# Linear attention's score and output products in another order: lower and upper 64 rows of the array take turns

## The reference, cut to what matters

```
att = jnp.einsum('bthk,bshk,btshk->bhts', qc, kc, jnp.exp(rel))
o = jnp.einsum('bhts,bshv->bthv', att, vc) + jnp.einsum('bthk,bhkv->bthv', qc * jnp.exp(cum), s)
```

## Time and profile before

| | |
|---|---|
| median of 3 runs | 1804.55 us (1803.39 to 1806.12) |
| span of the profiled execution | 1801.9 us |
| PE busy | 1703.9 us (95%), 10222 records |
| PEld busy | 1453.3 us (81%) |
| DVE busy | 1345.6 us (75%) |
| ACT busy | 847.1 us (47%) |
| moved by all transfers | 245.90 MB, mean 136 GB/s |

### The profile page before, as it was taken

How to read it: one execution, slowest core, us unless ns; L and a number is a source line. 1 busy time by engine, 2 the same in 40 slices (tenths; PEclk the granted TensorE clock), 3 DMA queues, 4 the chain that set the end, 5 groups by cost and what they waited for, 6 DMA issues and landing times. The chain is left out here.

```text
span 1801.9 us, 26476 instructions
## 1 busy us (share of the span) xinstructions
PE 1703.9 (95%) x10222; PEld 1453.3 (81%) x10222; DVE 1345.6 (75%) x2521; ACT 847.1 (47%) x1476; POOL 55.0 (3%) x113
## 2 busy tenths in 40 slices
PE   4899999898999999999999998999998999999997
PEld 3788887676888888877788766988898888989997
DVE  6677874775999999977975578699975555765594
ACT  2623334745444442245553565333344467665541
POOL 0910000000000000000000000000000000000000
PEclk9999999999999999999999999999999999999998
DMA  8343432031222225743453332554455454444552
GB/s 318 118 143 115 130 128 70 1 125 63 94 94 95 97 97 195 246 158 117 159 182 115 120 106 95 176 175 152 152 187 190 135 179 143 129 129 129 152 160 87
DMA packets 70150, 245.90 MB, mean 136 GB/s; under 512 B 7951, under 2 KB 9480, under 8 KB 69768
## 3 DMA queue, kind: packets, MB, share of 16 engines
q1 hardware_dynamic: 68024, 241.52, 41.2%
q10 hardware_dynamic: 2000, 2.69, 0.5%
HBM read 242.80 MB, written 1.11 MB: 135 GB/s over the span
## 5 line engine op out<-in xcount | busy, mean ns | idle before, releaser
L462 PE MATMUL banks<-m,weights_high 128*128 128x256 f32 (+1 forms) x4336 | 1042.3, 334 | 33.1 <-DVE weights_low L498 24.9
L462 PEld LDWEIGHTS banks<-m,weights_high 128*128 128x128 f32 x4336 | 734.9, 191 | 125.3 <-issue 23.3
L462 PE MATMUL banks<-m,weights_low 128*128 128x256 f32 (+1 forms) x2168 | 715.3, 330 | 0.0
L498 DVE TENSOR_TENSOR weights_low<-weight_ring,weights_high 128x1024 fp32r<-128x1024 f32 x293 | 355.8, 1224 | 225.1 <-ACT weights_high L493 224.1
L462 PEld LDWEIGHTS banks<-m,weights_low 128*128 128x128 f32 x2168 | 414.2, 191 | 38.3
L493 ACT ACTIVATE weights_high<-weight_ring 128x1024 fp32r<-128x1024 f32 x293 | 308.9, 1056 | 233.7 <-PE banks L462 153.2
L630 DVE SCALAR_TENSOR_TENSOR m<-m,columns 128x189 f32<-128x189 f32 (+4 forms) x856 | 322.0, 456 | 25.0 <-ACT m L570 24.9
L769 DVE SCALAR_TENSOR_TENSOR m<-weight_ring,m 128x1024 bf16<-128x1024 f32 x184 | 225.2, 1224 | 17.9 <-DMA weight_ring<-in_weights 12.1
L569 ACT ACTIVATE m<-banks,columns 128x512 f32<-128x512 f32 (+1 forms) x120 | 83.1, 692 | 305.3 <-PE banks L462 305.2
L462 PE MATMUL banks<-m,weight_ring 128*128 128x256 f32 x704 | 152.1, 379 | 0.0
L462 PEld LDWEIGHTS banks<-m,weight_ring 128*128 128x128 f32 x704 | 133.9, 190 | 17.9
(11 more groups left out here) (393 smaller groups left out, 1600.7 us busy)
## 6 DMA issues: line engine op xcount, KB each, us to landing
weight_ring<-in_weights SPq DMA_DIRECT2D x433, 512.0 KB, 3.7
m<-entering SPq DMA_DIRECT2D x32, 256.0 KB, 3.2
x<-in_tokens SPq DMA_DIRECT2D x1, 2048.0 KB, 13.9
m<-in_cmp_w SPq DMA_DIRECT2D x1, 2048.0 KB, 7.4
m<-in_cond SPq DMA_DIRECT2D x2, 512.0 KB, 4.7
out<-x ACTq DMA_DIRECT2D x8, 128.0 KB, 1.9
columns<-in_columns SPq DMA_DIRECT2D x1, 633.0 KB
m<-in_rg_w ACTq DMA_DIRECT2D x1, 512.0 KB, 3.4
```

Source lines behind the costliest of these rows:

```text
L462: mm = pe.matmul(out, lhsT, rhs, start=p.start and i == 0, stop=p.stop and i == len(passes) - 1)
L498: dve.tensor_tensor(w_lo[:, g % PARTS, :], K.ring[:, PLACE[PRODUCT_BLOCKS[g]] % RING, :], w_hi[:, g % PARTS, :].bitcast(F32), ALU.subtract ...
```

## The change

The score products of one call are issued in two halves of eight. Within a half each product of the lower rows is followed by the one of the upper rows of the same chunk and pair, which goes into the next bank. The output products are issued for each chunk and pair of heads: first the two products over 128 rows, one for each head, then the state's products, lower and upper rows by turns. The products themselves, their operands, the places they write, the semaphores and all other engines' code are the same; the accumulation in each place begins with the same product as before.

```
         def scores(q, k):
-            for i in range(4):
-                r = slice(GK * (i % 2), GK * (i % 2) + GK)
+            for half in range(2):
                 for j in range(4):
-                    c, pair = 2 * (i // 2) + j // 2, j % 2
-                    mm = pe.matmul(K.bank[:, B + i, j * P:j * P + P], k[r, pair, c * P:c * P + P],
-                                   q[r, pair, c * P:c * P + P], start=True, stop=True)
+                    c, pair = 2 * half + j // 2, j % 2
+                    for i in range(2):
+                        r = slice(GK * i, GK * i + GK)
+                        mm = pe.matmul(K.bank[:, B + 2 * half + i, j * P:j * P + P], k[r, pair, c * P:c * P + P],
+                                       q[r, pair, c * P:c * P + P], start=True, stop=True)
             mm.then_inc(*self.scored.up())
...
             for c in (2 * half, 2 * half + 1):
-                for h in range(GH):
-                    mms = [(self.att[:, 4 * (h % 2 + 2 * (c // 2)) + 2 * (c % 2) + h // 2, :],
-                            f["gv"][:, c, h * GV:h * GV + GV])]
-                    r = slice(GK * (h % 2), GK * (h % 2) + GK)
-                    for d in range(2):
-                        pos = CHUNK_ORDER[d].index(c)
-                        if pos:
-                            i = 2 * d + h // 2
-                            mms.append((self.qc[r, i, c * P:c * P + P], self.state[r, i, pos - 1, :]))
-                    for j, (a, b) in enumerate(mms):
-                        at = (2 * (c % 2) + h // 2) * GV
-                        mm = pe.matmul(K.bank[:, B + 2 * half + h % 2, at:at + GV], a, b, start=(j == 0),
-                                       stop=(j == len(mms) - 1))
+                entered = [(d, CHUNK_ORDER[d].index(c) - 1) for d in range(2) if CHUNK_ORDER[d].index(c)]
+                for pair in range(2):
+                    at = (2 * (c % 2) + pair) * GV
+                    outs = [K.bank[:, B + 2 * half + u, at:at + GV] for u in range(2)]
+                    for u in range(2):
+                        h = 2 * pair + u
+                        mm = pe.matmul(outs[u], self.att[:, 4 * (u + 2 * (c // 2)) + 2 * (c % 2) + pair, :],
+                                       f["gv"][:, c, h * GV:h * GV + GV], start=True, stop=not entered)
+                    for n, (d, pos) in enumerate(entered):
+                        for u in range(2):
+                            r = slice(GK * u, GK * u + GK)
+                            mm = pe.matmul(outs[u], self.qc[r, 2 * d + pair, c * P:c * P + P],
+                                           self.state[r, 2 * d + pair, pos, :], start=False, stop=n == len(entered) - 1)
             mm.then_inc(*self.outs.up())
```

## The result

| | before | after |
|---|---|---|
| median of 15 runs | 1807.75 us (1801.43 to 1812.61) | 1797.39 us (1793.51 to 1802.77) |
| span of the profiled execution | 1801.9 us | 1798.3 us |

The ratio of after to before is 0.9945, with a 95% interval of 0.9934 to 0.9957: 0.55% faster, about 10 us. A second series gave 0.9943 (0.9925 to 0.9961). The forecast was 1793.3 us, a ratio of 0.9938 to the 1804.55 us of before.

The account below looks back on a forecast made before the run. PE was taken to bound the stage with the linear attention: 5.5 us from scores and 5.7 from outputs, 11.2 off the 1801.9 us span, gives 1790.7, plus 2.65 makes 1793.3 us; 8 in 10 from 1790.5 to 1800.

Parts of the forecast that it names:

- PE paces the stage: Linear attention stage: PE is busy throughout, so a microsecond of its work saved comes off the span; 11.2 us in sum.
- A scores call: Scores: with halves taking turns, first to last start takes 1.77 us instead of 2.55, so 0.78 us less a call.
- three records at each change: Scores before: 3 records at each of three half changes already run in the other half's shadow, 0.96 us a call.
- Six levels and the diagonal give, the last one doesn't: Scores: seven calls give 0.78 us each, 5.5 us; in the last level DVE's own chain delays the copy.
- The margin left in front of the copy: DVE's copy of the scores: of 0.88 us idle in six levels, 0.78 is needed and 0.10 stays.
- Outputs: Output products: 5.7 us less, of which 3.2 from 16 fewer changes of shape and 2.5 from pairing.
- the rule 0.11 n + 0.20: Outputs: cost in us of a part with n records in a stream, 0.20 being lost at each change of shape.
- Issue pace: Scores pairs need a record every 0.055 us; the skill page's 62 ns, giving 4.0 instead of 5.5, wouldn't bind.
- The slower rival: Scores and outputs: turns between halves cost what one stream costs; 4.1 us slower, 1808.7 us; chance 0.05.
- The absolute time: Whole kernel: median run of 1793.3 us, from a span of 1790.7; 8 in 10 from 1790.5 to 1800.
- the forecast's own range: Whole kernel: 1791.5 to 1795.5 us if the forecast holds (chance 0.75), as single runs lay up to 1.6 from their median.
- The 2.65 us added between span and run: Whole kernel: the median of runs before lay 2.65 us above the profiled span; the same was added to 1790.7.

Follow-up runs that it names:

- early_take: Changed kernel, but DVE takes the last level's scores one tick earlier; executed once, 1793.68 us.
- outputs_same_half: Changed kernel with outputs grouped by half instead of by pair, so the two halves never run together; executed once, 1799.44 us.
- both: Changed kernel with each output half's products over 128 rows first, then all over 64, and the last level's copy one tick earlier; 1793.07 us, ratio to before 0.9910.

## Why the prediction was right, point by point

- **PE paces the stage: right.** The stage gave back what PE's own work lost in seven calls and the outputs, 11.2 us at its last filler; only the last level's call gave nothing. Rows 3 name three waits; the view has a fourth, 0.3 us at L1927 for PE's sequencer, which stayed as it was.
- **A scores call: right in mechanism, 0.02 us off.** 0.76 instead of 0.78 us a call. The 1.77 us of the forecast is not what 15 steps of 0.11 and 0.10 make, 1.75; measured are 2.06 - 0.27 = 1.79. That three records at each change were already hidden before was read from the earlier trace rows; runs of 4, 8 and 16 confirm it. A reckoning that took the order before as fully serial, 3.51 us, would have promised 1.7 us a call (3.51 - 1.77).
- **Six levels and the diagonal give, the last one doesn't: right.** Levels 16.70 us apart; PE's wait before the last distances grew to 1.1 us on the weight load (0.4 before), where 1.2 was forecast. `early_take` shows that the place was named rightly. The margin left in front of the copy was forecast at 0.10 and is 0.15; that there are about 0.2 more behind the copy was not in the prediction.
- **Outputs: right.** 5.7 us by forecast; 2.4 + 3.3 by measure, and each half within 0.05 us of the rule 0.11 n + 0.20 in three new orders: the changed kernel's, `outputs_same_half`'s and `both`'s.
- **Issue pace: the rule did not bind.** A call of 32 products' records with their loads went through in 2.06 us, less 0.27 for the last: 0.058 us a record. The Trainium skill's 62 ns for each matmul would allow no less than 1.98 + 0.27 = 2.25 us, an estimate from that page ("TensorE: Matmul & The Clock Gate", "Back-to-back issue gap"). The page ties this pace to hardware decoding being off, and no run here shows which way the chip was set. The changed calls have the 64-row halves and the 128 moving columns at once, which rows 7 and 8 had only one at a time.
- **The slower rival** (halves that don't run together) would have had calls of 3.8 us. It would decide from a pair's step of 0.20 us on; the measured one is 0.11.
- **The absolute time: 4.1 us off,** within the range of 1790.5 to 1800 but outside the forecast's own range of 1791.5 to 1795.5. The forecast stood on three runs of before with a median of 1804.55; fifteen have 1807.75. Those 3.2 us are most of the miss, and the ratio, which doesn't depend on it, is 0.0007 off, inside its interval. The narrow range rested on the 1.6 us by which three runs lay from their median; the fifteen lie up to 6.3 us from theirs. The 2.65 us added between span and run compared a median with the span of one execution: within one execution of the changed kernel the two were 1.7 to 1.9 us apart (a run of 1799.98 us had a span of 1798.3). The last 0.9 us of the miss is as much as is lost between 794 and 808 us, which the prediction, with everything behind the stage shifted alike, had at nothing; that it is the same 0.9 isn't shown.

Left open: whether two halves that write the *same* bank would also pair. That order wasn't tried.

## What to carry to other kernels

Before promising what alternating array halves will bring, count how much the present order already overlaps: records in flight per slice show it, and here 9 of 16 possible steps were already hidden. Where products over 64 and over 128 rows mix, count the changes of shape as their own term; grouping by shape gave more than the pairing did in the outputs. After PE gets faster beside another engine, measure what is left of that engine's cover: a small addition that was free may now be on the path.

## What the runs showed of the hardware that was not expected

- About three records of 64 rows can be pending in one half while the other starts: runs of 4, 8 and 16 records took 2.16, 2.82 and 3.50 us for 32 records.
- A change between products over 128 and over 64 rows costs 0.20 us whichever way it goes, at full clock; a group of eight records over both halves takes 0.72 us, of one half 1.16.
- How often PE falls to the lower clock differs from one execution of the same kernel to the next (mean 0.982 and 0.987 in two profiles of the changed kernel, spans 1798.3 and 1791.4 us), enough to hide two thirds of a gain of 11 us when single profiles' spans are compared.
- One stretch at the lower clock, between 780 and 810 us, is in all eight profiles of kernels with new outputs and a new order of the scores (mean there 0.89 or 0.94), and in none of the four others (1.00). A change in one stage may so cost a little in a later one, here 0.9 to 1.1 us; why isn't shown.
